# An RWKV-7 scan with its transition matrices made ahead, in a two-layer hybrid encoder on one Trainium2 core

## What is computed

```python
def step(S, inp):
    r_t, w_t, k_t, v_t, kk_t, a_t = inp
    Skk = jnp.einsum('bhvk,bhk->bhv', S, kk_t)
    S = S * w_t[:, :, None, :] - Skk[..., None] * (kk_t * a_t)[:, :, None, :] + v_t[..., None] * k_t[:, :, None, :]
    return S, jnp.einsum('bhvk,bhk->bhv', S, r_t)
S, o = lax.scan(step, S0.astype(F32), xs)
```

## Time and profile before

| what | us |
|---|---|
| median of 3 runs | 1724.28 |
| lowest and highest run | 1716.37, 1726.32 |
| span of the profiled execution | 1725.6 |
| mixing stage, layer 0, inverses to last retention product | 413.3 to 476.0 |
| the same in layer 1 | 1266.9 to 1329.55 |

### The profile page before, as it was taken

How to read it: one execution, slowest core, us unless ns; L and a number is a source line. 1 busy time by engine, 2 the same in 40 slices (tenths; PEclk the granted TensorE clock), 3 DMA queues, 4 the chain that set the end, 5 groups by cost and what they waited for, 6 DMA issues and landing times. The chain is left out here.

```text
span 1725.6 us, 27385 instructions
## 1 busy us (share of the span) xinstructions
PE 1635.1 (95%) x11276; PEld 1471.4 (85%) x11276; DVE 867.9 (50%) x1240; ACT 593.6 (34%) x871; POOL 196.7 (11%) x129
## 2 busy tenths in 40 slices
PE   7999999789999999999989999997899899999997
PEld 6999989688752989999979999897887439899997
DVE  4555335966252345553555543279662524455535
ACT  4334334421021344432444333443210314433333
POOL 1000027440010000000000000474201100000000
PEclk9999989898565799999989999998875758999999
DMA  7444424320010234444434444242201001444443
GB/s 287 165 155 168 171 97 155 115 101 4 7 56 25 74 125 167 170 161 157 149 127 170 168 155 164 98 148 102 95 5 31 32 25 74 171 160 157 169 174 127
DMA packets 32035, 209.81 MB, mean 122 GB/s; under 512 B 4392, under 2 KB 6072, under 8 KB 7752
## 3 DMA queue, kind: packets, MB, share of 16 engines
q1 hardware_dynamic: 29392, 200.39, 32.3%
q0 software_dynamic: 2560, 8.26, 1.4%
HBM read 204.54 MB, written 4.10 MB: 121 GB/s over the span
## 5 line engine op out<-in xcount | busy, mean ns | idle before, releaser
L792 DVE TENSOR_TENSOR split_w<-wc,split_w 128x2048 fp32r<-128x2048 f32 x140 | 320.6, 2292 | 373.8 <-ACT split_w L519 373.8
L519 ACT ACTIVATE split_w<-wc 128x2048 fp32r<-128x2048 f32 x140 | 268.3, 1917 | 539.0 <-PE bank L1252 341.2
L1246 PE MATMUL bank<-split_x,split_w 128*128 128x288 f32 x2816 | 398.3, 299 | 15.2 <-ACT split_x L525 15.2
L1246 PEld LDWEIGHTS bank<-split_x,split_w 128*128 128x128 f32 x2816 | 385.4, 190 | 20.1 <-issue 12.7
L1269 PE MATMUL bank<-split_x,split_w 128*128 (+1 forms) x2112 | 282.2, 295 | 0.0
L1269 PEld LDWEIGHTS bank<-split_x,split_w 128*128 128x128 f32 x2112 | 281.8, 188 | 0.0
L1252 PE MATMUL bank<-split_x,split_w 128*128 128x288 f32 x1408 | 202.2, 296 | 0.2 <-DVE split_w L792 0.2
L1252 PEld LDWEIGHTS bank<-split_x,split_w 128*128 128x128 f32 x1408 | 192.6, 189 | 0.4 <-DVE split_w L792 0.4
L419 POOL TENSOR_TENSOR split_x<-wc,split_x 128x1024 fp32r<-128x1024 f32 x32 | 79.6, 2487 | 509.1 <-ACT split_x L563 509.1
L563 ACT ACTIVATE split_x<-wc 128x1024 fp32r<-128x1024 f32 x62 | 65.4, 1058 | 113.3 <-PE bank L1323 113.3
L1320 PE MATMUL bank<-split_h,split_x 128*128 128x288 f32 x496 | 84.8, 314 | 7.5 <-ACT split_h L568 7.4
(11 more groups left out here) (291 smaller groups left out, 1838.9 us busy)
## 6 DMA issues: line engine op xcount, KB each, us to landing
wc<-wcol SPq DMA_DIRECT2D x174, 1024.0 KB, 4.8
wc<-wfirst SPq DMA_DIRECT2D x12, 1024.0 KB, 5.0
con<-consts_in SPq DMA_DIRECT2D x1, 2230.0 KB
arena<-kc_in POOLq DMA_DIRECT2D x8, 256.0 KB, 3.3
arena<-vc_in POOLq DMA_DIRECT2D x2, 1024.0 KB, 5.1
xT<-x_in SPq DMA_DIRECT2D x2, 576.0 KB, 4.5
k_out<-zT POOLq DMA_DIRECT2D x8, 144.0 KB, 2.2
v_out<-zT POOLq DMA_DIRECT2D x8, 144.0 KB, 2.3
```

Source lines behind the costliest of these rows:

```text
L519: act.activation(ws[s % 2][0], wc[:, p % RING, :], ACT.Copy).then_inc(S["cast"], 1)
L792: dve.tensor_tensor(lo, wc[:, (POS_FFN[f] + s) % RING, :], hi, ALU.subtract).then_inc(S["wlo"], 1)
L1246: pe.matmul(o, hi[:, k, cs], x[:, k, :], start=(w == 0 and k == 0), stop=False)
```

## The change

A chunk is one affine map of the state: new state = transition matrix times old state, plus an input. The changed kernel makes both for all nine chunks ahead of the scan.

- The inverse is applied to the decayed keys with tokens as output rows (`atok` in place of `atT`).
- 36 products of 32 rows by 64 outputs give the part of the transition matrices that is not the plain decay; ScalarE copies them to `mt`. 72 more give the inputs; VectorE copies them to `kv`. The four chunks of a tile read the four row quarters and write four banks.
- A step of the scan is one group of products `mt` times state, and one addition by VectorE; the decayed old state is added to `kv` meanwhile. The sample's chunk shares the first step with chunk 0, so there are eight steps.
- `read_with` folds `atok` into the reading vectors, so that an output needs the state at its chunk's start and `u0` as it was before the scan. `out_within` makes the part of the outputs within chunks, `out_across` the part from the states. All but the last pieces of these, and the retention pieces, stand between the steps. `ret_kv` and the retention states on VectorE move to the end.
- Products of the two row halves alternate instead of following each other by halves, in the decay products, the scores and the outputs. The two halves of the new groups write one bank, in different partitions.

```diff
-                    for i in range(NCH):
...
-                        for g in range(4):
-                            hp, b = head_of(g)
-                            mm = pe.matmul(bank[g // 2][rows, HD * b:HD * b + HD], atT[hp:hp + 64, b, CH * i:CH * i + CH],
-                                           st[hp:hp + 64, s_at, b, :], start=True, stop=True)
-                        mm.then_inc(S["u_ps"], 1)
+                    order = [(j, b, e) for j in range(3) for b in range(2) for e in range(2)]
+                    for j, b, e in order:
+                        hs, g = slice(64 * e, 64 * e + 64), 2 * e + b
+                        for q in range(TILES[j][1] // CH):
+                            rows, at = slice(CH * q, CH * q + CH), 128 * j + HD * b
+                            mm = pe.matmul(bank[4 + q][hs, at:at + HD], atok[rows, j, HD * g:HD * g + HD],
+                                           tok[rows, j, 2 + b, hs], start=True, stop=True)
+                    mm.then_inc(S["mh_ps"], 1)
...
+                    with_step = {0: [(read_with, 0), (read_with, 1), (read_with, 2)], 1: [(out_within, 1)],
+                                 2: [(out_within, 0)], 3: [(ret_tok, 0), (ret_scores, 0)],
+                                 4: [(out_within, 2), (ret_tok, 1)], 5: [(ret_scores, 1), (ret_tok, 2)],
+                                 6: [(ret_scores, 2), (out_across, 0)],
+                                 7: [(ret_kv, 0), (ret_kv, 1), (ret_kv, 2), (ret_kv, 3), (ret_kv, 4)]}
+                    done = 0
+                    pe.wait_ge(S["hc"], 4)
+                    for step, chunks in enumerate(SCAN):
+                        pe.wait_ge(S["mtc"], min(step + 1, 4))
+                        if step:
+                            pe.wait_ge(S["s_ok"], done)
+                        for at_, i in enumerate(chunks):
+                            j, q = chunk(i)
+                            done += 1
+                            for b in range(2):
+                                for e in range(2):
+                                    hs, m = slice(64 * e, 64 * e + 64), MT_AT[q] + 128 * j + HD * b
+                                    mm = pe.matmul(bank[(step + at_) % 2][hs, HD * b:HD * b + HD], mt[hs, m:m + HD],
+                                                   st[hs, i if i < 8 else 9, b, :], start=True, stop=True)
+                            mm.then_inc(S["s_ps"], 1)
+                        for also, which in with_step.get(step, ()):
+                            also(which)
+                    pe.wait_ge(S["s_ok"], 9)
+                    out_across(1)
+                    out_across(2)
                     pe.wait_ge(S["rsd"], 10)
                     pe.wait_ge(S["smd"], 6)
...
+                    def out_across(j):
+                        n = TILES[j][1]
+                        pe.wait_ge(S["rp_ok"], j + 1)
+                        pe.wait_ge(S["owc"], 3)
+                        for b in range(2):
+                            for q in range(n // CH):
+                                i = 4 * j + q
+                                for e in range(2):
+                                    hs, at = slice(64 * e, 64 * e + 64), n * b + CH * q
+                                    mm = pe.matmul(bank[O_BANK[j]][hs, at:at + CH], st[hs, i if i < 8 else 9, b, :],
+                                                   ar[hs, b, 1, CH * i:CH * i + CH], start=True, stop=True)
+                        mm.then_inc(S["o_ps"], 1)
```

On VectorE a step is now this, with `kv` in place (`h`):

```diff
+                            for b in range(2):
+                                h = kv[:, at + HD * b:at + HD * b + HD]
+                                chained(dve.scalar_tensor_tensor(h, st[:, old, b, :], einc[:, b, end:end + 1], h,
+                                                                 ALU.mult, ALU.add))
...
+                            dve.tensor_tensor(st[:, new, :, :], ms, kv[:, at:at + 128].rearrange("p (b n) -> p b n", b=2),
+                                              ALU.add).then_inc(S["s_ok"], 1)
```

More of the change, by code:

```diff
@@ L286, in pa, with chunk @@
             return par[rows, a:a + 1]
+        def chunk(i):
+            return (i // 4, i % 4) if i < 8 else (2, 0)
         def mats_psum(j, e):
@@ new lines, in _ @@
+                    for j, b, e in order:
+                        hs, g = slice(64 * e, 64 * e + 64), 2 * e + b
+                        at = 128 * j + HD * b
+                        for q in range(TILES[j][1] // CH):
+                            rows = slice(CH * q, CH * q + CH)
+                            pe.matmul(bank[q][hs, at:at + HD], tok[rows, j, 4 + b, hs], tok[rows, j, 6 + b, hs],
+                                      start=True, stop=False)
+                        for q in range(TILES[j][1] // CH):
+                            rows = slice(CH * q, CH * q + CH)
+                            mm = pe.matmul(bank[q][hs, at:at + HD], tok[rows, j, 2 + b, hs],
+                                           u0[rows, j, HD * g:HD * g + HD], start=False, stop=True)
@@ L1510, in _, with read_with @@
+                    mm.then_inc(S["mh_ps"], 1)
+                    def read_with(j):
+                        n = TILES[j][1]
+                        pe.wait_ge(S["mtc"], j + 1)
                         for b in range(2):
                             for e in range(2):
-                                hs = slice(64 * e, 64 * e + 64)
-                                pe.matmul(bank[2 + b][hs, 0:HD], tok[rows, j, 4 + b, hs], tok[rows, j, 6 + b, hs],
-                                          start=True, stop=False)
@@ L1515, in _, with out_within @@
-                        pe.wait_ge(S["u_ok"], 2 * i + 2)
+                                g = 2 * e + b
+                                mm = pe.matmul(bank[4 + j][64 * e:64 * e + 64, n * b:n * b + n],
+                                               atok[0:n, j, HD * g:HD * g + HD], ctm[0:n, j, 128 * g:128 * g + n],
+                                               start=True, stop=True)
+                        mm.then_inc(S["rp_ps"], 1)
+                    def out_within(j):
+                        n = TILES[j][1]
+                        if j == 2:
+                            pe.wait_ge(S["owc"], 2)
@@ L1516, in _ @@
                         for b in range(2):
                             for e in range(2):
-                                hs = slice(64 * e, 64 * e + 64)
-                                g = 2 * e + b
-                                mm = pe.matmul(bank[2 + b][hs, 0:HD], tok[rows, j, 2 + b, hs],
-                                               u0[rows, j, HD * g:HD * g + HD], start=False, stop=True)
-                            mm.then_inc(S["s_ps"], 1)
-                        for step, which in with_chunk.get(i, ()):
-                            step(which)
+                                hs, g = slice(64 * e, 64 * e + 64), 2 * e + b
```

253 lines of the change are left out of this document (135 added, 118 removed).

## The result

The changed kernel takes 1665.66 us (median of 4 runs, 1663.68 to 1666.95) where the kernel before takes 1724.57 (4 runs): a ratio of 0.966, 95% interval 0.9635 to 0.9681. The profiled spans are 1725.6 and 1663.9 us.

A forecast was written before the change was run, and what follows sets the result against it. TensorE, busy 95% of the span, was taken as the bound. Parts of 5.8 + 11.3 + 25.4 + 2.9 + 7.3 = 52.7 us replace 62.7 per layer, 20 us less in all: 1704 us, range 1685 to 1724.

The forecast's parts named there:

- inverses: Applying the inverse matrices, per layer: wider second products and ScalarE's wider last copy raise 4.6 to 5.8 us.
- Part 2: Transition matrices and inputs made ahead: 216 recorded products at 0.044 us, 9.5, plus 1.8 for VectorE's copies: 11.3 us per layer.
- Part 3: Scan of eight steps, with retention and output pieces between them: 25.4 us per layer against 26.7.
- Part 5: Retention outputs, both halves mixed: 7.3 us per layer against 12.6.
- rival (c): Upper clock holds through products ahead, scan and retention outputs: 18 us more saved per layer, 1668 us; chance 0.08.
- the terms for read_with and out_within: New work between the scan's steps, priced at the lower clock: read_with 2.8 us, out_within 5.9 us per layer.
- The wait in the step before the last: In the scan, the third scores wait for VectorE's masks of the second, behind that step's addition: 1.2 us.
- The wait for VectorE's copies: Ahead of the scan, TensorE waits for all four of VectorE's copies of the inputs: 1.8 us.
- Part 4: Tail behind the scan: out_across of two tiles (2.5 us) beside VectorE's ten retention states, 2.9 us before TensorE goes on.
- Rival (a): Row halves writing one bank wait for each other in steps, out_across and retention outputs: 9.7 us lost, 1724; chance 0.22.
- Rival (b): The 216 products made ahead don't overlap: 0.124 us each, 26.8 us, layer 7.3 us longer, 1739 us; chance 0.12.
- 2 us per layer: Behind the mixing stage: the clock's return falling earlier or later in the work can move each layer by about this.

The follow-up runs named there:

- run 4: Kernel before with two unread full-array products (128 rows, 128 outputs, 384 columns) added behind each of the nine scan chunks: 1730.83 us, ratio 1.0039.
- run 8: Kernel before with two unread quarter-array products (64 rows, 64 outputs, 384 columns) added behind each scan chunk: 1762.37 us, ratio 1.0235.
- run 3: Kernel before with RWKV and retention outputs alternating between the two halves of the heads, scan as before: 1691.06 us, ratio 0.9815.
- run 7: Changed kernel with unread full-array products added in three of TensorE's waits (three, two and three, 256 columns): 1658.05 us, ratio 0.9626.
- run 5: Changed kernel with the 216 recorded products made ahead ordered one row quarter after the other, not side by side: 1671.74 us, ratio 0.9699.
- run 2: Changed kernel with out_within and the first tile's out_across moved from between the steps to behind the scan: 1672.26 us, ratio 0.9699.
- run 1: Changed kernel with products of one half ahead of the other's in steps, read_with, out_within, out_across and retention outputs: 1691.29 us, ratio 0.9814.
- run 14: The kernel of run 10 with unread full-array products, two ahead of the scan and two ahead of the last readings: 1652.04 us, ratio 0.958.
- run 10: Changed kernel with ScalarE making two of the four input copies, and VectorE's masks and retention states moved earlier: 1663.9 us, ratio 0.9657.
- run 6: Changed kernel with VectorE copying the chunks' inputs four times over, so TensorE waits longer ahead of the scan: 1672.46 us, ratio 0.9694.

## Why the prediction was wrong

The parts, first layer, forecast and measured: inverses 5.8 and 5.3, products ahead 11.3 and 6.4, scan 25.4 and 15.0, tail 2.9 and 2.8, retention outputs 7.3 and 5.0; in all 52.7 and 34.5.

**The step that failed is the choice of the clock.** All prices in parts 2, 3 and 5 were taken at the lower level, and rival (c), which takes the upper, got 0.08. Where the forecast has 0.50, the trace shows 0.90 and 0.74 in the two scans and 0.71 and 1.00 in the retention outputs. (c) gave 1668 and 34.8 us per layer (52.7 - 17.9); measured were 1665.66 and 34.5 and 36.1. That it comes so close is in part luck: its products ahead come to 9.1 us, its scan to 13.3 and its retention outputs to 3.7, where the first layer has 6.4, 15.0 and 5.0. The argument against it was that the old output windows are busy without a gap and yet at 0.50. Runs 4 and 8 show what is wrong with it: busy time says nothing about how much of the array has work. The program's own shapes did: 64 or 128 rows by 64 outputs, one half at a time. The Trainium skill (TensorE: Matmul & The Clock Gate, Part 1) has the clock released by sustained busy time. Run 8 disagrees: 79.4 of 80.6 us busy, at 0.50. Whether rows or outputs count, and why run 3's outputs, with both halves at work, stayed at 0.50 when the scan of the changed kernel did not, is open.

**Part 3, sizes.** By their own products the terms for read_with and out_within are 2.7 and 6.0, not 2.8 and 5.9; the sum is the same. At 0.50 the forecast's prices hold or are a little high: the step's products take 0.62 us as forecast, `read_with` 2.47 (2.8 forecast), a tile of `out_within` 1.96 (1250.07 to 1252.03; 16 x 0.148 = 2.37). The wait in the step before the last was forecast at 1.2 and is 1.12. At 1.00 the step with its tile takes 1.46 instead of 2.58. An estimate of the whole scan at 0.50: run 7's 13.67 us at 1.00, less 1.1 of added work, times 2.58 / 1.46, plus that wait, gives 23.3. So of the 10.4 us missed some 8 are clock and 2 are price.

**Part 2, the price.** Here it is the size of the term: 0.044 was taken from half rows, and 0.015 came out (3.19 us of busy TensorE for 216). Run 5 shows that it is mostly the four quarters side by side: in turn at 0.50 they cost 0.043. The clock is a smaller share, since in the first layer of run 2 they ran side by side at 0.50 for 0.016 each (1.78 / 113), against 0.011 at 1.00 in the changed kernel:

```profile
417.50:419.28 1.78, 1.78 (x113) 1.78 (x108) 0.00 (x0) 1.26 (x4) 0.31 (x1) 0.50 0.31 81
```

The wait for VectorE's copies is 1.71 us (1.8 forecast), and a hole of 1.53 us that nobody forecast makes up the 6.4.

**Part 4 held.** 2.9 forecast, 2.84 measured, the wait for VectorE's retention states (1.49 us) in it. **Part 5** was a little high at its clock: 7.3 forecast, 6.40 at 0.50 in run 2, 3.92 at 1.00 in the second layer.

**Rival (a) fell.** The readings of the states give all four cases: 0.124 in turn at 0.50, 0.071 in turn at 1.00 (run 4, same line), 0.0625 side by side in two banks at 0.50 (run 3), 0.030 side by side in one bank at 1.00. No cost of the one bank shows: the last is half of the one before it, at twice the clock. The Trainium skill (TensorEngine Tiling (Array Packing), Restrictions and Gotchas) says that different row tiles cannot access the same PSUM bank at the same time; as a cost it does not show in these rows. **Rival (b) fell** with run 5: even in turn the price stays below its 0.090.

**What made the 59 us.** Runs 1 and 3 split the stage nearly evenly: 62.7 with neither, 48.1 with alternating outputs in the old kernel, 48.0 re-associated with halves in turn, 34.5 with both. Each of these figures contains the clock as it then fell, so the split is one of edits, not of mechanisms. The prediction had allowed 2 us per layer for the work outside the stage, and 7.0 us came from there. They can't be put down to the change: outside the stage the profiled executions of all these runs take 1585.6 to 1600.2 us, though next to nothing is edited there, and the kernel before is the longest of them (run 8, the same kernel with work added in the stage: 1587.4).

## What to carry to other kernels

Count how much of TensorE's array a stretch fills before choosing the clock that prices are taken at: a stretch that is busy but uses a half or a quarter of the array may run at the lower clock, and an edit that fills it can win more than the instructions it saves. When a forecast's terms all rest on one granted clock, sum them once at the other and give that sum a real chance. Small products of different row quarters and output halves, interleaved one by one, cost about half of what they cost in turn, and added products that nobody reads, in waits alone, can make a kernel faster (run 14 against run 10).

## What the runs showed of the hardware that was not expected

- Useless work paid: 1652.04 us with two pairs of added products (run 14) against 1663.9 for the same kernel without them (run 10). A quarter-array control was run only for the waits of run 7, and gave nothing (1666.78).
- TensorE stood still for 1.53 us within the 216 products, with no semaphore behind it. The row of the changed kernel:

```profile
420.34 0.21 PE L1563 MATMUL bank<-extra 32*64 32x64 f32 x1 [1.53 <-issue]
```

  It is 1.47 to 2.04 us where that stretch ran at 1.00, 0.56 to 0.82 where it ran at 0.50, and absent in run 5, whose products are slower. What it waits for was not tried. The trace has one packet of 0.02 MB on an instruction queue between 417.5 and 418.0 us, ahead of the hole; whether TensorE ran out of instructions is not shown.
- A longer wait (run 6) cost less than its own 5.9 us in one layer and more in the other.
